# Six value units with both weight parts behind one load of the high tokens

## What is computed

```
v = h @ w            # h: 256 tokens x 1024, w: 1024 x 512, out: 256 x 512 values
o = softmax(q k^T) @ v
```

## Time and profile before

| | |
|---|---|
| median of 3 runs | 1657.73 us |
| the runs | 1656.03, 1657.73, 1659.61 us |
| span of the profiled execution | 1659.8 us |
| TensorE matmul busy | 1357.1 us (82%) |
| TensorE weight loads busy | 1079.8 us (65%) |
| VectorE busy | 643.6 us (39%) |
| ScalarE busy | 489.9 us (30%) |
| matmuls of the six value units | 288 of 14402 |

### The profile page before, as it was taken

One profiled execution on the slowest core, in us unless ns is written; L12 is line 12 of the kernel. 1 busy time (PEld: TensorE's weight loads), 2 busy tenths in 40 slices (PEclk: granted clock), 3 DMA queues, 4 the chain that ended last, 5 costly groups with the idle time before them and its releaser, 6 DMA issues.

```text
span 1659.8 us, 32820 instructions
## 1 busy us (share of the span) xinstructions
PE 1357.1 (82%) x14402; PEld 1079.8 (65%) x14402; DVE 643.6 (39%) x1008; ACT 489.9 (30%) x819; POOL 0.2 (0%) x4
## 2 busy tenths in 40 slices
PE   8999999999999999998875766765585676567666
PEld 8998899999999999996543433433343343344333
DVE  6787735878787778663110100101110010111001
ACT  5766466456554455432000000000000000000001
POOL 0000000000000000000000000000000000000000
PEclk9999999999999999999998988988898898899889
DMA  7442023453446665488999999999999999999997
GB/s 300 160 146 102 27 102 104 176 195 136 177 180 243 229 246 193 150 350 362 428 425 432 426 429 434 429 428 428 430 429 430 431 429 425 432 430 429 428 431 321
DMA packets 41401, 517.93 MB, mean 312 GB/s; under 512 B 4720, under 2 KB 4848, under 8 KB 6384
## 3 DMA queue, kind: packets, MB, share of 16 engines
q1 hardware_dynamic: 41184, 516.71, 75.9%
q10 hardware_dynamic: 144, 0.17, 0.0%
HBM read 515.81 MB, written 1.05 MB: 311 GB/s over the span
## 4 chain that ended last, share of the span: by engine, by line
PE 47%; DMA 42%; DVE 6%; ACT 3%; issue 1%; SPq 1%; another core or an unknown queue 0%; DVEq 0%; ACTq 0%; PEldq 0%
DMA e_gu<-experts 41%; PE psum L323 10%; PE psum L324 9%; PE psum L325 9%; PE psum L887 6%; PE psum L928 3%; DVE w_low L1555 1%; DMA w_raw<-dense 1%; PE psum L541 1%; PE psum L383 1%; ACT w_high L1001 1%; PE psum L934 1%; PE psum L525 1%; PE psum L392 0%; PE psum L898 0%
## 5 line engine op out<-in xcount | busy, mean ns | idle before, releaser
L887 PE MATMUL psum<-e_gu,x_xt 128*32 128x256 f32 x3072 | 220.0, 450 | 172.7 <-DMA e_gu<-experts 172.7
L887 PEld LDWEIGHTS psum<-e_gu,x_xt 128*32 128x32 f32 x3072 | 109.4, 129 | 276.2 <-DMA e_gu<-experts 184.8
L323 PE MATMUL psum<-h_high,w_high 128*128 128x256 f32 x896 | 256.9, 287 | 4.6 <-DVE h_low L1519 3.6
L324 PE MATMUL psum<-h_low,w_high 128*128 128x256 f32 x896 | 253.7, 283 | 0.0
L325 PE MATMUL psum<-h_high,w_low 128*128 128x256 f32 x896 | 253.5, 283 | 0.0
L1555 DVE TENSOR_TENSOR w_low<-w_raw,w_high 128x2048 fp32r<-128x2048 f32 x100 | 228.5, 2288 | 38.0 <-ACT w_high L1001 33.0
L1001 ACT ACTIVATE w_high<-w_raw 128x2048 fp32r<-128x2048 f32 x100 | 191.2, 1914 | 71.4 <-PE psum L325 54.4
L2206 DVE COPY x_yb<-psum 128x256 f32<-128x256 f32 x64 | 27.2, 425 | 419.7 <-PE psum L928 419.7
L323 PEld LDWEIGHTS psum<-h_high,w_high 128*128 128x128 f32 x896 | 170.9, 191 | 6.1 <-issue 3.8
L324 PEld LDWEIGHTS psum<-h_low,w_high 128*128 128x128 f32 x896 | 171.2, 191 | 0.4 <-issue 0.2
L325 PEld LDWEIGHTS psum<-h_high,w_low 128*128 128x128 f32 x896 | 170.9, 191 | 0.0
(11 more groups left out here) (447 smaller groups left out, 2162.0 us busy)
## 6 DMA issues: line engine op xcount, KB each, us to landing
e_gu<-experts SPq DMA_DIRECT2D x44, 4096.0 KB, 52.9
w_raw<-dense SPq DMA_DIRECT2D x100, 1024.0 KB, 4.8
e_dn<-experts SPq DMA_DIRECT2D x46, 2048.0 KB, 49.4
e_dn<-experts SPq DMA_DIRECT2D x36, 1024.0 KB, 54.8
e_gu_lo<-experts SPq DMA_DIRECT2D x16, 2048.0 KB, 51.5
e_gu_hi<-experts SPq DMA_DIRECT2D x16, 2048.0 KB, 55.9
e_gu<-experts SPq DMA_DIRECT2D x8, 1024.0 KB, 8.1
e_gu<-experts SPq DMA_DIRECT2D x2, 2560.0 KB, 10.3
```

Source lines behind the costliest of these rows:

```text
L323: mm(ps, w[0], src[0], start=start, stop=False, **kw)
L324: mm(ps, w[0], src[1], start=False, stop=False, **kw)
L887: last = mm(half(psum[32 * s:32 * s + 32, GU_BANK[j % 2], 0:256], P), X["xt"][:, k, CAP * j:CAP * (j + 1)], expert_gu(j, k)[:, :, s * P:(s ...
```

## The change

`unit_tok` gives way to `unit_tok_wide` at the six value units; the values of the second block (`v2`) stay as they were. The rings of low and high weight parts become one tensor, so that a strided view takes the low and the high part of a unit as one operand of 512 columns. For each token tile and chunk there are two matmuls: low tokens by high weights (256 columns) and high tokens by low and high weights (512 columns). That makes 32 loads and 32 matmuls a unit, with as many columns in all. Low results land in region 0 of a bank, high ones in region 1, and each token tile takes a bank of its own. ScalarE copies region 1 to SBUF (`value_low`), VectorE adds region 0 to it and releases the bank (`values`). The products with the values wait for a count of these additions. ScalarE's copies of `fox_v` move from behind the roots to ahead of them.

```diff
+            def unit_tok_wide(name, src=HI):
+                pe.wait_ge(sem("w_low"), ORDER[name] + 2)
+                w = both(name).rearrange("p a (k n) -> p a k n", k=DC)
+                for t in range(TT):
+                    ps = half(proj.fill(pe, f"{name}.{t}"))
+                    for k in range(DC):
+                        tok_high, tok_low = chunk_of(src, k, slice(t * P, (t + 1) * P))
+                        mm(ps[:, 0, :], tok_low, w[:, 1, k, :], start=(k == 0), stop=False, skip_group_check=True)
+                        last = mm(ps, tok_high, w[:, :, k, :], start=False, stop=(k == DC - 1), skip_group_check=True)
+                    proj.filled(last, f"{name}.{t}")
+                done[name] = proj.full(f"{name}.{TT - 1}")
...
# mem_pv on TensorE
+                if hd % 2 == 0:
+                    pe.wait_ge(sem("values"), 8 + 2 * (hd // 2 + 1))
...
# ScalarE
+            def value_low(name, u, dst):
+                for t in range(TT):
+                    ps = half(proj.wait(act, f"{name}{u}.{t}"))
+                    ac(dst[:, t, u * 256:(u + 1) * 256], ps[:, 1, :], ACT.Copy).then_inc(sem("value_low"), 1)
...
+            for u in range(2):
+                ahead(f"fv{u}")
+                value_low("fv", u, A["fox_v"])
             for j, nm in enumerate("qk"):
-                ahead(f"fv{j}")
                 for hd in range(H):
                     root(f"fss_{nm}{hd}", sq[:, j * H + hd, :])
-            for u in range(2):
-                ps = half(proj.wait(act, f"fv{u}"))
-                proj.emptied(ac(A["fox_v"][:, :, u * 256:(u + 1) * 256], ps, ACT.Copy), f"fv{u}")
-                ahead(f"fv{u}")
...
# VectorE
             lows("sq1")
+            def values(name, u, dst):
+                for t in range(TT):
+                    ps = half(proj.wait(dve, f"{name}{u}.{t}"))
+                    n_values[0] += 1
+                    dve.wait_ge(sem("value_low"), n_values[0])
+                    o = dst[:, t, u * 256:(u + 1) * 256]
+                    link(V.tensor_tensor(o, ps[:, 0, :], o, ALU.add))
+                    proj.release(dve, f"{name}{u}.{t}")
+                    dve.sem_inc(sem("values"), 1)
+            values("fv", 0, A["fox_v"])
...
+            values("fv", 1, A["fox_v"])
             fox_norm("q", A["st"][:, 24:25], range(H))
...
                 between()
+                if 1 <= lv < 3:
+                    values("sv", lv - 1, A["sb_v"])
...
             lows("mv1")
+            values("mv", 0, M["v"])
             mem_max(2); mem_max(3)
             lows("mo_0")
             mout(0); mout(1)
             mem_norm_p(2); mem_norm_p(3)
             lows("mo_1")
+            values("mv", 1, M["v"])
             mout(2); mout(3)
```

More of the change, by code:

```diff
@@ L283, in high, with both @@
         def high(name):
-            return w_high[:, ORDER[name] % HIGH, :]
+            return w_parts[:, RAW + ORDER[name] % HIGH, :]
         def low(name):
-            return w_low[:, place(name), :]
+            return w_parts[:, place(name), :]
+        def both(name):
+            lo, hi = place(name), RAW + ORDER[name] % HIGH
+            return w_parts[:, lo:hi + 1:hi - lo, :]
         NORMS = ("mix", "mem", "xq", "ffn", "n1", "n2", "final")
@@ L441, in _ @@
                 aux.filled(last, f"decay{q}")
-            unit_tok("fv0"); unit_tok("fv1")
+            unit_tok_wide("fv0"); unit_tok_wide("fv1")
             head_sums("fss_q", "fox_sq", lambda hd: sq[:, hd, :], T)
@@ L492, in pv @@
                 pe.wait_ge(sem(ready), hd + 1)
+                if name in ("fpv", "spv") and hd % 2 == 0:
+                    pe.wait_ge(sem("values"), 4 * (name == "spv") + 2 * (hd // 2 + 1))
                 mm(ps[:, 0:T], v[:, 0, hd * P:(hd + 1) * P], pt[:, hd % 2, 0:T], start=True, stop=False,
@@ L500, in sb_scores @@
                 if hd == 0:
-                    pe.wait_ge(sem("sb_qkv"), 6)
+                    pe.wait_ge(sem("sb_qk"), 4)
                 q, k = A["sb_q"][:, hd, :], A["sb_k"][:, hd, :]
@@ L607, in _ @@
                 elif lv < 3:
-                    unit_tok(f"sv{lv - 1}")
+                    unit_tok_wide(f"sv{lv - 1}")
                 between()
@@ L696, in _ @@
             query_sums(1)
-            unit_tok("mv0", hm)
+            unit_tok_wide("mv0", hm)
             mem_turn(0); mem_turn(1)
@@ L700, in _ @@
             mem_pv(0); mem_pv(1)
-            unit_tok("mv1", hm)
+            unit_tok_wide("mv1", hm)
             mem_turn(2); mem_turn(3)
@@ L1102, in _ @@
                 ac(sq[:, H + hd, :], A["fox_k"][:, hd, :], ACT.Square).then_inc(sem("fox_sq"), 1)
+            for u in range(2):
+                ahead(f"fv{u}")
+                value_low("fv", u, A["fox_v"])
             for j, nm in enumerate("qk"):
-                ahead(f"fv{j}")
                 for hd in range(H):
                     root(f"fss_{nm}{hd}", sq[:, j * H + hd, :])
-            for u in range(2):
-                ps = half(proj.wait(act, f"fv{u}"))
-                proj.emptied(ac(A["fox_v"][:, :, u * 256:(u + 1) * 256], ps, ACT.Copy), f"fv{u}")
-                ahead(f"fv{u}")
             def sb_evac(u):
                 nm = ("sq", "sk", "sv")[u // 2]
+                if nm == "sv":
+                    value_low("sv", u % 2, A["sb_v"])
+                    ahead(f"sv{u % 2}")
+                    return
                 ps = half(proj.wait(act, f"{nm}{u % 2}"))
[L1115 to L1119, removed]
+                c = slice(2 * (u % 2), 2 * (u % 2) + 2)
+                link(ac(A["sb_q" if nm == "sq" else "sb_k"][:, c, :], ps, ACT.Copy, scale=SCALE if nm == "sq" else 1.0))
                 proj.release(act, f"{nm}{u % 2}")
-                act.sem_inc(sem("sb_qkv"), 1)
+                act.sem_inc(sem("sb_qk"), 1)
                 ahead(f"{nm}{u % 2}")
@@ L1284, in _ @@
                 ahead(f"mq{u}")
-            def mem_values(u):
-                ps = half(proj.wait(act, f"mv{u}"))
-                proj.emptied(ac(M["v"][:, :, u * 256:(u + 1) * 256], ps, ACT.Copy), f"mv{u}")
             rq = M["st"][:, 16:16 + TT * H]
@@ L1307, in _ @@
             ahead("mq1")
-            mem_values(0)
+            value_low("mv", 0, M["v"])
             ahead("mv0")
@@ L1313, in _ @@
             mem_exp(3)
-            mem_values(1)
+            value_low("mv", 1, M["v"])
             turned("mpt", 2, M["pt"], 512, "mem_pT")
@@ L1663, in _ @@
             lows("sq1")
+            n_values = [0]
+            def values(name, u, dst):
[8 more added lines that the diff above has]
+            values("fv", 0, A["fox_v"])
             def fox_norm(nm, gain, heads):
```

3 lines of the change are left out of this document (1 added, 2 removed).

## The result

The changed kernel takes 1666.1 us (median; runs of 1665.7, 1666.0, 1666.2 and 1667.1) where the kernel before takes 1658.6 beside it: a ratio of 1.0047, 95% interval 1.0035 to 1.0059, so 5.8 to 9.8 us slower. Measured again later, it gave 1.0046 (1.0032 to 1.0059). The forecast was 1662.9 with a range to 1665.3: the right way, too small, and outside the range. The profiled execution has a span of 1665.4 us and took 1667.1, so 1.7 us lie outside a span.

A forecast was written before the change was run, and what follows sets the result against it. TensorE was taken to bound the dense part, transfers the expert stream after it. Lateness after sv 0.5, memory values 3.1 and a clock fall 1.6 sum to 5.2 us; on the median 1657.7 that gives 1662.9, range 1659.2 to 1665.3.

The forecast's parts named there:

- the one before sq0: At fv, sq0 waits for VectorE's addition to release its bank, about 1.1 us; sq0 starts 1.2 us late.
- the rival on the other side: At mem_pv of head 2, VectorE's additions are covered and TensorE does not wait: 1656.3 us, chance 0.10.
- the memory values: At mv, mem_pv of head 2 waits for mv1's additions behind VectorE's full chain: 3.1 us late, bounds 2.6 and 3.6.
- The gain of a pair: At the value units, a 256- plus a 512-column product saves 18 ns over three of 256: 0.29 us a unit.
- rival 4: At the value units, a 512-column product costs two of 256, so no gain in sv: 1663.5 us, chance 0.04.
- rival 5: At the value units, a 512-column product costs no more than one of 256 (0.117 us): 1659.7 us, chance 0.02.
- The wait for the bank: At fv1, TensorE waits 0.4 us until ScalarE has copied fk0 out of its bank, contained in the delay of sq0.
- sv0 1.1 us late: At the start of sv0, VectorE's late norms and reciprocals delay the solve, so sv0 begins 1.1 us late.
- The fall behind mem_pv: In the wait before mem_pv of head 2, idle TensorE lets its clock fall: 1.6 us lost, bounds 0 and 3.2.
- rival 1: At the mem_pv wait, the clock holds and only 0.5 + 3.1 us are lost: 1661.3 us, chance 0.29.
- my five stretches: Weak TensorE work in the dense part (from 28, 95, 237, 257, 278 us), each followed by a clock fall.
- (d): At fv, VectorE's fox_norm and ScalarE's first root are queued later: root ends at 117.7, reciprocals begin 3.2 us late.

The follow-up runs named there:

- three of 256: Changed kernel with each 512-column product split again into two of 256 into the same regions (48 loads a unit): 1665.6 us, ratio 1.0036 to the kernel before.
- changed again: The changed kernel, unmodified, measured a second time in more rounds: 1666.7 us, ratio 1.0046 to the kernel before.
- mv1 added first: Changed kernel with VectorE's additions of mv1 moved ahead of the low weights of mo_1: 1664.7 us, ratio 1.0031 to the kernel before.
- bank wait alone: Kernel before with one wait added: fv1 waits until ScalarE has released the bank of fk0: 1660.7 us, ratio 1.0012.
- fillers: Changed kernel with small unread bf16 products in TensorE's new waits before fv1 and mem_pv of heads 0 and 2: 1664.1 us, ratio 1.0035 to the kernel before.
- fk copied early: Changed kernel with ScalarE's copies of fk0 and fk1 ahead of the eight exponentials: 1663.9 us, ratio 1.0030 to the kernel before.

## Why the prediction was off

**Right.** The places, the engines and the order of the waits, all but the one before sq0 (1.1 us forecast, none in the first trace, 0.35 in the second); that the gain doesn't reach the end; and the rival on the other side fell by the reason given, VectorE's full chain. At the memory values the forecast was 3.1 us and the trace shows 3.4; mem_pv waited 1.07 and 2.80.

**The gain of a pair.** I took 18 ns from the nearest row. Over the units it is 3 to 6: the row was a float32 pass, and a split product costs 0.46 ns a column at any width from 256 up. The row nearest in kind was the earlier trace rows, and its 10 ns over 256 columns had to be read as a rate, not as a gap. It is a small term: the forecast counted 0.6 us of it. So rival 4 had the mechanism right (512 columns cost two of 256) and rival 5 had it wrong, though the miss of the time doesn't come from here.

**The wait for the bank.** This step failed in its size. I had 0.4 us, contained in what follows. It was 1.82, since fv0 ended at 105.5 and not at 106.9. The trace before had its clock low up to 104.3, and I took that as given; in the trace after it rose at 101.9. That is a term sized from one state of a clock which differs from run to run. I had sv0 1.1 us late: it is 0.9 late where the clock is low that long, and 2.4 where it rises by 102.9, since the wait then takes what the clock gives. Behind waits of 1.7 to 1.8 us at this place the clock fell in two of five traces (changed and three of 256; not in changed again, mv1 added first and bank wait alone).

**The fall behind mem_pv.** This step failed. I expected the clock to fall in a wait of 2.9 us behind transposes. The window of the changed kernel within the wait:

```profile
422.00:423.00 1.00, 0.00 (x0) 0.00 (x0) 1.00 (x1) 0.68 (x2) 0.00 (x0) 1.00 0.89 164
```

TensorE does nothing and the granted clock is 1.00, and mo starts at full clock. None of the five traces with this wait of 2.8 us shows a fall there, so the 1.6 us are nothing, as rival 1 said. I had made a rule of five falls in one trace, and other traces of the same code have stretches without one. Length, which rival 1 named, doesn't explain it alone. Four of my five stretches were longer (3.25 to 3.75 us), but the fifth was as short as this wait, and the clock fell behind it at 281.8 (trace before):

```profile
278.53 0.33 PE L576 MATMUL psum<-a_gdn_qk,a_state 128*128 128x64 f32 x2
...
281.34 0.38 PE L323 MATMUL psum<-yc_high,w_high 128*128 128x256 f32 x1
```

Why the clock held in the wait is open.

**The sum and its base.** The two traces differ by 5.6 us (1665.4 and 1659.8), close to the forecast's 5.2, but by chance, for it is made up otherwise: from fv0 to sv0 it is 3.0 us longer (55.4 against 52.4), of which the waits make 2.2 (3.1 against the 0.9 of the kernel before) and the granted clock, low at other times, the rest; fv0 began 0.7 earlier, 1.8 of the 2.3 at sv0 are left at the memory scores, the memory part adds 3.4, and 0.4 comes behind it. The medians differ by 7.5. The profiled execution before, with 1.7 us outside its span, would stand at 1661.5, at the upper end of its runs and 2.9 us above the median; that of after stands 1.0 above its own. I had set the span beside the times and called the distance 2.1. If falls of the clock make up these distances, the median execution before had one or two fewer than the trace on which I built, and that of after at most one fewer than its own. The range did not reach to that case. It doesn't follow from its own terms either: rival 1 with the lower bounds gives 1657.7 - 0.2 + 2.6 = 1660.1 and not 1659.2, the forecast with the upper bounds 1657.7 + 1.1 + 3.6 + 1.6 = 1664.0 and not 1665.3. Two smaller sums are off too: the terms named under (d) give 117.2 for the first root and not 117.7 (the 0.4 us at the bank belong in between; with them it fits the 117.6 of the second measurement), and 422.8 less 419.6 is 3.2.

**What stays open.** The two traces differ by 5.6 us, and the waits make as much (2.2 and 3.4). Traces with like clocks give nearly the same: 2.4 us at fv, some 0.5 back between sv0 and the memory scores (0.4 of it with three of 256 too, so not by the width), 3.4 in the memory part, 5.3 in all. The medians differ by 7.5. That the rest, some 2 us, is about one fall of the clock more in the usual run agrees with the steps in the runs, with the kernel with fillers and with that with fk copied early, and isn't shown: the timed runs carry no trace.

## What to carry to other kernels

Before loads are saved on TensorE, look at what its products cost a column: where 512 columns cost twice what 256 do, a wider product gives nothing back. An addition at the copy out of PSUM puts a second engine between a product and its reader. Read in that engine's timeline what stands ahead of it there; here 0.42 us of work cost up to 0.73 of its time, and four such additions 3.4 us of TensorE's. A wait that is priced in one trace is priced in one state of the clock: look for other traces of the same code before it goes into a sum. And compare medians with medians: a profiled execution may be one or two falls of the clock away from them.

## What was not expected of the hardware

- A split product costs 112 ns for 128 columns, 117 for 256, 177 for 384 and 234 for 512 at the upper clock; a pass of an unsplit float32 product of 256 columns costs 216. At the lower clock 256 columns of a split product cost 213 ns, a cycle each, and 512 cost 426.
- Waits of 2.8 us with no work on TensorE left the granted clock at its upper level in all five traces that have one, while 2.8 us of 64-column products were followed by a fall at 281.8 us in the trace before. The same stretches of weak products were followed by a fall in some traces and not in others.
- The kernel before runs in steps of about 1.7 us (1656, 1658, 1660, 1661), on one chip and with nothing else changed. One fall of the clock costs 1.5 to 1.6 us.
